# Three edits in the attention layer of an fp32 kernel: sums of its block products in place, its output weights in four buffers, and another order of VectorE's steps

## The reference, cut to what matters

```python
def odd_layer(x, norm_g, w_in, b_forget, w_out):
    hn = rmsnorm(x, norm_g)
    proj = hn @ w_in                      # 2048 x (4 * 2048 + 16)
    q, k, v, z, f_logit = jnp.split(proj, cuts, axis=-1)
    log_f = jax.nn.log_sigmoid((f_logit + b_forget).astype(jnp.float32))
    o = forgetting_attention(q.reshape(shp), k.reshape(shp), v.reshape(shp), log_f)
    o = o * jax.nn.silu(z)
    return x + o @ w_out
# forgetting_attention, for one head and one block of 128 queries:
    s = jnp.einsum('bhqd,bkhd->bhqk', qi, k).astype(jnp.float32) * scale
    s = s + cqi[..., None] - cum[:, :, None, :]
    s = jnp.where(kpos[None, :] <= qpos[:, None], s, -jnp.inf)
    p = jax.nn.softmax(s, axis=-1).astype(v.dtype)
    return jnp.einsum('bhqk,bkhd->bqhd', p, v)
```

## Time and profile before

| | us |
|---|---|
| median of three runs (3011.49 to 3013.39) | 3012.54 |
| the profiled execution's own time | 3011.28 |
| its span, first to last instruction | 3009.4 |
| TensorE busy in it | 2894.2 (96%) |
| VectorE, ScalarE, GpSimd busy | 1594.5, 1302.0, 1432.3 |
| mean granted TensorE clock, share of full | 0.990 |

### The profile page before, as it was taken

One profiled execution on the slowest core, in us unless ns is written; L12 is line 12 of the kernel. 1 busy time (PEld: TensorE's weight loads), 2 busy tenths in 40 slices (PEclk: granted clock), 3 DMA queues, 4 the chain that ended last, 5 costly groups with the idle time before them and its releaser, 6 DMA issues.

```text
span 3009.4 us, 52820 instructions
## 1 busy us (share of the span) xinstructions
PE 2894.2 (96%) x20478; PEld 2433.6 (81%) x20478; DVE 1594.5 (53%) x2101; ACT 1302.0 (43%) x1777; POOL 1432.3 (48%) x1037
## 2 busy tenths in 40 slices
PE   8999999999999999999999999996999999999898
PEld 6777777777877887887787778875999999999787
DVE  7555565343444138777723352146777767777312
ACT  6433344255655233333335453234455454545422
POOL 1223332533245446666543334434666666666643
PEclk9999999999999999999999999998999999999999
DMA  5111111222123433222242234431223222222433
GB/s 216 57 59 58 58 58 58 94 74 82 58 84 109 147 115 112 91 93 92 101 137 91 84 112 133 146 106 64 95 98 103 100 100 102 94 94 98 147 124 117
DMA packets 98561, 298.17 MB, mean 99 GB/s; under 512 B 10608, under 2 KB 16880, under 8 KB 97408
## 3 DMA queue, kind: packets, MB, share of 16 engines
q1 hardware_dynamic: 71440, 246.12, 24.2%
q10 hardware_dynamic: 26992, 50.22, 4.9%
HBM read 273.45 MB, written 22.84 MB: 98 GB/s over the span
## 4 chain that ended last, share of the span: by engine, by line
PE 77%; DVE 10%; issue 6%; ACT 3%; POOL 2%; DMA 1%; DVEq 0%; ACTq 0%; POOLq 0%; SPq 0%
PE ps L338 8%; PE ps L340 8%; PE ps L339 8%; PE ps L2036 6%; PE ps L2039 6%; PE ps L2038 6%; PE ps L1028 4%; PE ps L1029 4%; PE ps L1030 4%; PE ps L1348 3%; PE ps L1350 2%; PE ps L1349 2%; POOL w_lo L3341 2%; DVE arena L3147 1%; PE ps L1413 1%
## 5 line engine op out<-in xcount | busy, mean ns | idle before, releaser
L3341 POOL TENSOR_TENSOR w_lo<-raw,w_hi 128x512 fp32r<-128x512 f32 x632 | 849.6, 1368 | 1243.4 <-ACT w_hi L761 1242.3
L338 PE MATMUL ps<-act_hi,w_hi 128*128 128x512 f32 x1232 | 485.9, 394 | 17.5 <-POOL w_lo L3341 12.5
L761 ACT ACTIVATE w_hi<-raw 128x1024 fp32r<-128x1024 f32 x320 | 337.4, 1055 | 361.9 <-PE ps L340 142.8
L340 PE MATMUL ps<-act_lo,w_hi 128*128 128x512 f32 x1232 | 480.4, 390 | 0.0
L339 PE MATMUL ps<-act_hi,w_lo 128*128 128x512 f32 x1232 | 480.1, 390 | 0.0
L2130 POOL TENSOR_TENSOR w_lo<-raw,w_hi 128x512 fp32r<-128x512 f32 x150 | 233.8, 1579 | 151.1 <-ACT w_hi L2053 151.1
L338 PEld LDWEIGHTS ps<-act_hi,w_hi 128*128 128x128 f32 x1232 | 231.6, 188 | 78.9 <-issue 22.7
L1028 PE MATMUL ps<-act_hi,w_hi 128*128 128x512 f32 x736 | 294.5, 400 | 0.0
L1029 PE MATMUL ps<-act_hi,w_lo 128*128 128x512 f32 x736 | 287.1, 390 | 0.0
L1030 PE MATMUL ps<-act_lo,w_hi 128*128 128x512 f32 x736 | 286.9, 390 | 0.0
L2130 POOL TENSOR_TENSOR w_lo<-arena,w_hi 128x512 fp32r<-128x512 f32 x150 | 223.5, 1510 | 121.0 <-ACT w_hi L2053 120.2
(11 more groups left out here) (492 smaller groups left out, 5979.9 us busy)
## 6 DMA issues: line engine op xcount, KB each, us to landing
raw<-stream SPq DMA_DIRECT2D x380, 512.0 KB, 3.3
arena<-stream SPq DMA_DIRECT2D x62, 512.0 KB, 3.3
residual<-mix ACTq DMA_DIRECT2D x32, 256.0 KB, 2.0
arena<-residual ACTq DMA_DIRECT2D x32, 256.0 KB, 2.7
arena<-x_rows SPq DMA_DIRECT2D x4, 1024.0 KB, 18.2
arena<-x ACTq DMA_DIRECT2D x16, 256.0 KB, 2.7
kept_qk<-mix ACTq DMA_DIRECT2D x16, 256.0 KB, 2.0
arena<-kept_qk ACTq DMA_DIRECT2D x16, 256.0 KB, 3.6
```

Source lines behind the costliest of these rows:

```text
L338: pe.matmul(dst, w_hi[:, slot, j, :], act_hi[:, a, :], start=first, stop=False)
L340: mm = pe.matmul(dst, w_hi[:, slot, j, :], act_lo[:, a, :], start=False, stop=last)
L761: nc.scalar.activation(w_hi[:, s, :, :], src[:, s % 2, :, :], ACT.Copy).then_inc(cast_done, 1)
L3341: last = nc.gpsimd.tensor_tensor(w_lo[:, s, part, :], raw[:, s % 2, part, :], w_hi[:, s, part, :].bitcast(F32), ALU.subtract)
```

## The change

- **Sums in place.** For this layer the norm leaves the activations unsplit in `mix`. The sums s1 to s4 are made there in place, so the eight additions of `fold_whole` go. s1 and s3 of the first quarters come right behind the norm, ahead of `first_vector`; ScalarE rounds only s1 and s2 of a quarter ahead of the weights of head 0's gate, and s4, s3 later; GpSimd takes the rests of s2 ahead of the loop's first weights, those of s4 behind it. VectorE splits q and k ahead of the first T1.
- **Output weights in four buffers.** The first four halves of the output weights are loaded into the loop's four weight buffers, each as soon as it is free, and are rounded and split in the order 2, 0, 3, 1 (`out3_cast`, `out3_gpsimd`); the heads' outputs come back into `arena` and `mix`.
- **VectorE's order in a unit.** First pair: T3, l2, maxima, T4, scaling becomes l2, maxima, T3, scaling, T4. Second pair: T3, l2 becomes l2, T3.

```diff
@@ norm_vector
+            if norm == 2:
+                dve.wait_ge(norm_lo, KT * (norm + 1))
+                fold_sums(dve, 0, "13")
             first_vector(dve, (0, N_U, N_F)[norm], norm)
@@
+        def fold_sums(dve, q, names):
+
+            x11, x21, x22, x12 = (four(s_raw[n], q) for n in "2314")
+            F, tt = fold_sum, nc.vector.tensor_tensor
+            for name in names:
+                if name == "1":
+                    F.mark(tt(x22, x21, x22, ALU.add), f"s1{q}")
...
+        def fold_round(act, name, q):
+            if name in "34":
+                act.wait_ge(pe_half, 2 * (N_ODD + 3) + 1)
+            fold_sum.wait(act, f"s{name}{q}", 0)
...
-        w7_prep = Steps(sem("w7_prep"), "T1 l1 T2 T3 l2 T4")
+        w7_prep = Steps(sem("w7_prep"), "T1 l1 T2 l2 T3 T4")
@@ w7_sync
             sp.wait_ge(split_done, 2 * N_OUT3)
-            sp.wait_ge(decay_stored, 16)
-            sp.wait_ge(evac_act, N_ODD + 1 - ODD_SHIFT)
@@
+        def out3_sync(sp, load_to):
+
+            last = W7_PAIRS - 1
+            w7_prep.wait(sp, "T3", last)
+            sp.wait_ge(w7_lo, 5 * last + 2)
+            load_to(OUT3_RAW[0], N_OUT3, 0).then_inc(out3_loaded[0], 16)
...
+            sp.wait_ge(w7_lo, 5 * last + 5)
+            load_to(OUT3_RAW[2], N_OUT3 + 1, 0).then_inc(out3_loaded[2], 16)
+            load_to(OUT3_RAW[3], N_OUT3 + 1, 1).then_inc(out3_loaded[3], 16)
...
@@ attention_scalar, last unit of the loop
                 cast_next(0)
+                if last:
+                    out3_cast(act, 2)
                 w7_out.wait(act, "c22", at_pair(u, 1))
...
+                        if f1 == 4:
+                            out3_cast(act, 0)
+                            out3_cast(act, 3)
                 out(1, "c21")
+                if last:
+                    out3_cast(act, 1)
@@ attention_vector
                 prepare(u, par, 0, "T2")
                 decayed(u)
-                prepare(u, par, 0, "T3")
                 prepare(u, par, 0, "l2")
                 largest(u)
+                prepare(u, par, 0, "T3")
+                scaled(u)
                 prepare(u, par, 0, "T4")
-                scaled(u)
...
                 prepare(u, par, 1, "T2")
+                prepare(u, par, 1, "l2")
                 prepare(u, par, 1, "T3")
-                prepare(u, par, 1, "l2")
                 gated(u, at_gate)
@@ forget_scalar
+            fold_round(act, "1", 0)
+            fold_round(act, "2", 0)
+            taken(act, N_ODD + 1, (N_ODD + 1) % 2,
+                  lambda: nc.scalar.activation(at_k_in, ps[:, (N_ODD + 1) % 2, :], ACT.Copy))
             fg.wait(act, "n", 0)
...
             act.dma_start(decays, at_cum[0:ODD_HEADS, :]).then_inc(decay_stored, 16)
-            fold_round(act, 0)
-            taken(act, N_ODD + 1, (N_ODD + 1) % 2,
-                  lambda: nc.scalar.activation(at_k_in, ps[:, (N_ODD + 1) % 2, :], ACT.Copy))
-            fold_round(act, 1)
```

More of the change, by code:

```diff
@@ new lines, in build_program, with four @@
+        fold_act = Steps(sem("fold_act"), "h10 h20 h11 h21 h40 h41 h30 h31")
+        fold_dve = Steps(sem("fold_dve"), "l10 l11 l30 l31")
+        fold_pool = Steps(sem("fold_pool"), "l20 l21 l40 l41")
+        for steps in (fold_sum, fold_act, fold_dve, fold_pool):
+            steps.start(0)
+        def four(view, q):
+            return view[:, 4 * q:4 * q + 4, :]
+        def fold_sums(dve, q, names):
[4 more added lines that the diff above has]
+                    F.mark(tt(x22, x21, x22, ALU.add), f"s1{q}")
+                elif name == "3":
+                    F.wait(dve, f"s1{q}", 0)
+                    F.mark(tt(x21, x11, x21, ALU.subtract), f"s3{q}")
+                elif name == "2":
+                    F.wait(dve, f"s3{q}", 0)
+                    F.mark(tt(x11, x22, x11, ALU.subtract), f"s2{q}")
+                else:
+                    F.wait(dve, f"s2{q}", 0)
+                    F.mark(tt(x12, x12, x11, ALU.subtract), f"s4{q}")
@@ L1954, in build_program @@
         W7_POOL = (0, 3, 4, 5, 6)
+        OUT3_RAW = [w7_raw[r] for r in (0, 2, 1, 3)]
+        OUT3_ORDER = (2, 0, 3, 1)
+        out3_loaded = [sem(f"out3_loaded{i}") for i in range(4)]
+        out3_hi = [sem(f"out3_hi{i}") for i in range(4)]
         x1, x5, x2 = (w7_x[:, j, :] for j in range(3))
@@ new lines, in out3_cast, with out3_gpsimd @@
+        def out3_cast(act, i):
+            act.wait_ge(out3_loaded[i], 16)
+            act.wait_ge(w7_pe, 7 * W7_PAIRS - (1, 0, 3, 2)[i])
+            nc.scalar.activation(w_hi[:, i, :, :], OUT3_RAW[i], ACT.Copy).then_inc(out3_hi[i], 1)
+        def out3_gpsimd(pool):
+            for i in OUT3_ORDER:
+                pool.wait_ge(out3_hi[i], 1)
+                for k0 in (0, HK // 2):
+                    part = slice(k0, k0 + HK // 2)
+                    last = nc.gpsimd.tensor_tensor(w_lo[:, i, part, :], OUT3_RAW[i][:, part, :],
+                                                   w_hi[:, i, part, :].bitcast(F32), ALU.subtract)
+                last.then_inc(split_done, 1)
@@ L2285, in last_unit @@
                 A.start(u)
-                for i in range(4):
-                    act.wait_ge(w7_pe, 7 * W7_PAIRS - (1, 0, 3, 2)[i])
-                    cast(act, 2 * N_OUT3 + i, i)
                 values(u)
@@ L2670, in build_program @@
         fg = Steps(sem("fg"), "y mn n e l ls cum")
-        fg_t = [slots(arena, 18 + j)[0:FR, :] for j in range(4)]
+        fg_t = [slots(arena, 7 + j)[0:FR, :] for j in range(4)]
         def forget_tensor(pe):
@@ L3312, in _, with load_to @@
             w7_sync(sp)
[L3313 to L3325 removed]
+            def load_to(place, n, h):
+                return sp.dma_start(place.rearrange("p k c -> p (k c)"), stream[n, h, :, :])
+            out3_sync(sp, load_to)
+            with sp.Fori(N_OUT3 + 2, N_TILES) as n:
                 for h in range(2):
```

198 lines of the change are left out of this document (87 added, 111 removed).

## The result

| | before | changed |
|---|---|---|
| median (us), four runs each | 3012.01 (3011.31 to 3013.39) | 3034.33 (3033.85 to 3038.65) |
| span of the profiled execution | 3009.4 | 3032.4 |
| TensorE busy | 2894.2 | 2912.9 |
| mean granted clock | 0.990 | 0.987 |

The account below looks back on a forecast made before the run. The prediction took TensorE, busy 96% of the span, as the bound and read its waits. From 3011.3 us, start -12, loop +30 and end 0 gave 3029 us, range 3018 to 3038.

Parts of the forecast that it names:

- Start, -12: Ahead of the loop: gate product without a gap, first scores waiting some 9 us; 12 us saved, bounds -20 and -8.
- First pair, "directly nothing": First half of a unit: exponentials 1.35 us later, scaling 1.5 us shorter, so no direct gain.
- Second pair, x1 1.1 us late in each unit, 16.5 us: Second pair, product 2: TensorE waits for x1 and loses 1.1 us in each of 15 units, 16.5 us.
- Feedback, the decays 1.0 us late, 14 us: Next unit: late GpSimd rests delay T1, T2 and the decays, lengthening the scaling's wait by 1.0 us in 14 units.
- Loop, +30 in all: All units: x1's lateness and the late decays together cost 30 us, bounds +16 and +42.
- End, 0: Output weights behind the loop: the output product's start hardly moves, 0 us, bounds -7 and +3.
- Rival 1: In the loop: its costs don't come and only the start counts, 2999 us; chance 0.20.
- decision point: Second pair: if the mix starts before 2349.6 in the unit shown, product 2 never waits and Rival 1 holds.

Follow-up runs that it names:

- e2: The changed kernel with the old order in the second pair alone (T3 ahead of l2); 3013.99 us, ratio 1.0007.
- e1: The changed kernel with VectorE's old order in both pairs; 2995.66 us, ratio 0.9946.
- e4: The changed kernel with the second pair's old order, and the first pair as T3, l2, maxima, scaling, T4; 2985.66 us, ratio 0.9910.
- e5: The changed kernel with 12 more TensorE transposes, results unused, ahead of its wait for the scaling in each unit; 3032.25 us, ratio 1.0072.
- e8: The changed kernel with ScalarE taking x1 and cast(1, 4) ahead of the wait for the mix and its store; 3029.23 us, ratio 1.0063.
- e12: e4 with the changed order of the second pair (l2 ahead of T3) on top; 3004.40 us, ratio 0.9980.
- e3: The changed kernel with the old order in the first pair alone, l2 still ahead of T3 in the second; 3045.13 us, ratio 1.0108.
- e10: e4 with ScalarE taking c21 ahead of the last roundings at the end of the loop; 2985.95 us, ratio 0.9913.
- e9: e1 with ScalarE doing the exponentials ahead of cast(0, 5); 2978.53 us, ratio 0.9888.
- e7: The changed kernel with ScalarE doing the exponentials ahead of cast(0, 5); 3050.17 us, ratio 1.0134.

## Why the prediction was right, and where its steps were not

The forecast of 3029 us was 5 under the result, on the right side, with the result inside its range. The start came as forecast in the main. The loop's sum came near by luck, from terms that the runs don't bear out. Point by point:

- **Start, -12.** Measured -12.4. T2 was to come at 2065.7 and came at 2066.10; the gap ahead of the gate product is gone. The wait ahead of the first scores was to be 9 us and is 5.6: q and k are split by 2058.3 and not 2060, and the first T1 then took 3.38 us beside GpSimd, which gave the difference back.
- **First pair, "directly nothing".** This step failed. The scaling does shrink from 2.77 to 1.27 us, but the first exponential is 2.57 us later against the scores and not 1.35: l2, in T3's place, meets GpSimd (2.32 us and not the 1.33 taken over from T3), and the decays are 0.3 us late. A unit's wait grows by 0.9 us. With this pair's order alone (e2) the kernel is 18 us above e1, where the forecast had nothing directly. The cause is T3 behind the maxima, which makes late the cast that ScalarE has to do ahead of the exponentials: e2 and e4 differ in T3's place alone, and by 28 us. With T3 back, T4 behind the scaling is a gain of 10 us (e4 against e1).
- **Second pair, x1 1.1 us late in each unit, 16.5 us.** The delay was right: x1's wait is 1.08 us where the clock is full, and e5 shows it in all units. That it sets the time was wrong. In 10 units the half clock took its place; e5 shows that neither is in the sum, and in e8 x1's wait is gone and only 5 us come back. What the second pair's order costs in the changed kernel is 1.4 us on the ring (22.15 to 23.55), between e2 and the changed kernel 20 us, and e12 shows the same 1.4 on another first pair. e3 shows the price, 3.5 us a unit, where the lateness reaches T3 and the scaling: +49.5 us. Of the 3.5 us some 1.4 are the half clock, in the units that have it.
- **Feedback, the decays 1.0 us late, 14 us.** The way was right (GpSimd's rests, the next T1, T2, the decays with no idle time ahead of them), the size 0.3 us. It is not a term beside x1's wait but the same ring.
- **Loop, +30 in all.** Measured +33.3. The terms 16.5 and 14 came near it for a wrong reason: TensorE's waits were added up, where one had to ask which chain closes a unit: TensorE's before (47.98, with about 1 us of room in the ring), the ring after (50.62). That is 2.64 us a unit, in 14 periods 37, less 1.5 for the shorter first and last period (50.08, 49.90 us), and less the 2.2 by which the 14 periods of before (673.9 us) exceed 14 x 47.98, for the most part its two units with a half clock.
- **End, 0.** Measured +1.95, and -1.2 in e1 (55.34 us from the 15th unit to the last head, 56.53 before), but e5, with the changed order, has 56.57 (57.17 in e8), so at most a part of these 3 us is the order's. The granted clock in the 15 us from the output product's start is 0.82 in the changed kernel and 0.92 in e5; the rest stays open. The start of the output product was laid to the third split half; e10 agrees, since it starts no earlier with c21 out of the way and then waits by name for a split. So the visible wait for c21 costs nothing there.
- **Rival 1** (2999, the loop's costs don't come) is what e1 gives with the old order, 2995.7. Its decision point, the mix in time and x1 with it, was the wrong place: in e2 and e8 x1 is never waited for, and a unit still takes 49.2 and 50.2 us. What decides is T3 behind the maxima in the first pair and l2 ahead of T3 in the second.

What was not foreseen at all is the half clock behind the scaling's wait, which two units of before already had. In the changed kernel it cost nothing. In e3, where the way from the scaling to A leads over TensorE, it did: of the second to the 13th period the two with a full clock behind the wait took 50.08 us each, the others 51.3 to 52.8.

## What to carry to other kernels

When several engines in fixed order feed each other, find the ring before adding up waits: follow one step of one unit to the same step of the next without the engine that counts. Look whether any step of it waits for that engine. If none does, as in the changed kernel, its length is the time, and the waits of the main engine only trade places; if one does, as the decays do in the kernel before, the unit is closed over the main engine and that idle time is the ring's room. What follows a wait of the main engine, here the half clock, can be tested cheaply by filling the wait with spare work. That doesn't test the wait itself, whose end stays where it is.

A step on VectorE that works in SBUF has no price of its own while GpSimd runs beside it. Moving a step by 1 us is worth what it then meets: the same edit on ScalarE's list (exponentials first) gave -17 us on one order (e9) and +16 on another (e7).

## What the runs showed of the hardware

- A VectorE instruction of 128x1024 with two inputs in SBUF that takes 1.22 us alone takes 2.3 where it starts beside a GpSimd one (T3 in e3 and e4), and four scalings that take 1.27 together take 2.32, 2.77 or 4.59 in e9, before and e3. The maxima take 1.67 us in all of these. That agrees with the lock that the Trainium skill describes (SBUF — State Buffer, Who interferes with whom).
- Waits of the same 2.80 us are followed by a clock of 0.57 to 0.67 over 4 us in some units and of 1.00 in others, and waits of 1.90 us have been followed by 0.67 once in the kernel before and by 0.66 once in e1. With TensorE busy for half of the wait (e5, 1.5 us idle) it did not happen in 15 units. What decides it stays open here.
